# The last down projection in two column halves, with seven block products instead of eight in 15 of its 44 blocks

## The chip, the cores and the metric

One core of one Trainium2 chip runs the whole program once. The metric is the device time of one execution in microseconds (us); lower is better. The engines are called TensorE (PE in rows), VectorE (DVE), ScalarE (ACT), GpSimd (POOL) and SyncE (SP, which issues the DMAs of the weight stream).

## The reference

Two transformer blocks run over 256 tokens of width 2048, all in float32. The change lies in the end of the second block: the down projection of the SwiGLU, the residual addition and the final norm.

```python
def swiglu(h, w_in, w_down):
    gu = h @ w_in
    gate, up = jnp.split(gu, 2, axis=-1)
    return (jax.nn.silu(gate) * up) @ w_down
...
        x = x + swiglu(rmsnorm_2(x, norm_ffn_g[layer]), w_ffn_in[layer], w_ffn_down[layer])
    return rmsnorm_2(x, norm_final_g)
```

The hidden activation is 256 x 5632 and the weight `w_down` is 5632 x 2048, so the product sums over 44 slices of 128 rows.

## The kernel before

**The weight stream.** All weights are read once from HBM as one stream of pieces of 128 x 1024 float32 (512 KB). SyncE loads them in a fixed order into six raw buffers (`raw`, `RR` = 6). A buffer is loaded again when the piece that it held has been split.

**The split.** TensorE multiplies in a shortened form of float32 (`F32R`). Each piece is therefore split into two parts: ScalarE copies it into the shortened form (`split_hi`, line 444), and VectorE subtracts that from the original (`split_lo`, line 460). Both parts lie in a ring of four places (`ring`, `R` = 4). ScalarE waits for `weights_used` before it writes a place again, VectorE waits for `hi_ready`, TensorE waits for `lo_ready`. Activations are split in the same way: `hid2` holds both parts of the hidden activation.

**A block product.** `tokens` (lines 515 to 519) computes 128 tokens x 512 columns over 128 rows of the weight in three matmuls: low activation by high weight, high by low, high by high. The three lines 517, 518 and 519 are one matmul each.

**The last down projection (`down2`).** It takes 88 pieces. A piece holds two slices of 128 rows (`k`) and 512 of the 2048 columns, which makes it a *column quarter* `q`. Before, the quarters come one after the other: 22 pieces of quarter 0, then 22 of quarter 1, and so on. TensorE makes four block products for each piece, two slices by two halves of the tokens (`tt`), and sums into PSUM bank `2 * q + tt`. Piece by piece it waits for `lo_ready`. In the last quarter the last three pieces (`BY_TOKEN`) are taken for the first token half and then for the second, so that the first half can be finished earlier. TensorE also transposes the residual `x` into token order in between (`turn_x`), and ScalarE copies it out (`copy_turned`).

**After each quarter** VectorE adds the sum onto the residual in token order (`onto_tokens`, line 1742), ScalarE squares it for the norm (`square_tokens`, line 1160), and VectorE multiplies by the gain (`gained`, line 1747). These steps stand between calls of `split_lo` and `split_hi` in each engine's own order, which is written out by hand. Every engine works strictly in that order. The other engines tell each other by counting semaphores.

**GpSimd** has 30 instructions in the whole program, all in the first stage: squares of the context (lines 713 and 716), its scaling (line 722) and sums of squares (lines 726 and 730). It does nothing in the last stage.

Of the kernel before, what the change touches and what calls it, by code (L numbers as in the profile page):

```python
# [13 lines left out]
P = 128  # L14
D = 2048
T = 256
# [118 lines left out]


# [74 lines left out]
def two_blocks(nc, stream, cvec_d, c_bc_d, vecs_d, xc_d, x_d, rpb, w_fnet, base_tab, rope_tab, dft_tab, na_mask,  # L211
               stick_tab, dist_tab, g_bc_d, out_d):
    ctx = ExitStack()
    with ctx:
# [106 lines left out]
        pair2, _ = place("pair2", [P, KT, 2, T], F32R, reg)  # L321

# [80 lines left out]
        out_act, out_dve = sem("out_act"), sem("out_dve")  # L403

# [20 lines left out]
        def split_view(part, c, k, n):  # L425
            if by_tile(c):
                return split_tiles(part, c).rearrange("p (k m) n -> p k m n", k=k)
            return whole(part, c).rearrange("p (k n) -> p k n", k=k)

# [114 lines left out]
        def _(e):  # L544
# [158 lines left out]

        RES = {"out": 0, "down": 16, "out2": 32, "down2": 48}
# [26 lines left out]


        @block.scalar
        def _(e):
# [421 lines left out]
            def square_tokens(q, tt):  # L1156
                e.wait_ge(tok_y, 4 * q + 2 * tt + 1 if q < 3 else 13 + tt)
                if q:
# [4 lines left out]
            b, size = BASE["down2"], FT // 2  # L1163
            e.preload_act_table_set("sqrt_and_others")
            split_hi(e, b + LEAD + CPG, b + LEAD + 10)
            for n in range(4):
# [3 lines left out]
            split_hi(e, b + LEAD + 10, b + LEAD + 16)  # L1170
            for n in range(4, 8):
                copy_turned(n)
            at = b + LEAD + 16
            for q in range(3):
                to = b + (q + 1) * size + LEAD + 4
                split_hi(e, at, to)
                at = to
                for tt in range(2):
                    square_tokens(q, tt)
            split_hi(e, at, N_CHUNKS)  # L1180
# [12 lines left out]
        def _(e):  # L1193
# [544 lines left out]

            def onto_tokens(q, tt):
                e.wait_ge(tok_act, 2 * q + tt + 1)  # L1740
# [4 lines left out]
            def gained(q, tt):  # L1745
                e.wait_ge(tok_y, 4 * q + 2 * tt + 1)
# [3 lines left out]
            b, size = BASE["down2"], FT // 2  # L1750
            split_lo(e, b + LEAD + CPG, b + LEAD + 10)
            e.wait_ge(r_turned, 2)
            e.tensor_copy(small[:, 0:2], ps[:, 3, 0:2]).then_inc(r_copied, 1)
            at = b + LEAD + 10
            e.wait_ge(r_copied, 2)
            for q in range(3):
                to = b + (q + 1) * size + LEAD
                split_lo(e, at, to)
                at = to
                e.wait_ge(weights_used, b + (q + 1) * size)  # L1760
                if q == 0:
                    e.wait_ge(s_tables2, 48)
                for tt in range(2):
                    onto_tokens(q, tt)
                    split_lo(e, at, at + 1)
                    gained(q, tt)
                    split_lo(e, at + 1, at + 2)
                    at += 2
            split_lo(e, at, N_CHUNKS - 8)
# [6 lines left out]
            split_lo(e, N_CHUNKS - 8, N_CHUNKS)  # L1776
            for tt in range(2):
                if tt == 0:
                    e.wait_ge(column_done, COLUMN["down2"] + 1)
# [13 lines left out]
        def _(e):  # L1793
# [614 lines left out]
            def turn_x(n0):  # L2408

                e.wait_ge(sums_ready, SUMS["down2"])  # L2410
                if n0 == 0:
                    e.wait_ge(rinv_ready, NORM["ffn2"][2] + 1)
                    for tt in range(2):
                        m = e.matmul(ps[:, 3, tt:tt + 1], rinv[:, 0, tok(tt)], ident[:, 0:1], start=tt == 0, stop=True,
                                     skip_group_check=True)
                    m.then_inc(r_turned, 1)
                for n in range(n0, n0 + 4):
                    q, tt, bank = turned_at(n)
                    if n >= 4:
# [5 lines left out]
            def down_product(q, c, k, kt, tt):  # L2425
                return tokens(e, ps[:, 2 * q + tt, :], split_view(HI, c, 2, GW)[:, k], split_view(LO, c, 2, GW)[:, k],
                              hid2[:, kt, 0, tok(tt)], hid2[:, kt, 1, tok(tt)], kt == 0, kt == FT - 1)

            size = FT // 2
            for q in range(4):  # L2430
                if q == 0:
                    e.wait_ge(sums_ready, SUMS["down2"] - 4)
                elif q == 1:
                    e.wait_ge(r_copied, 2)
                elif q == 2:
                    e.wait_ge(tok_act, 8)
                for ch in range(size - (BY_TOKEN if q == 3 else 0)):
                    c = BASE["down2"] + q * size + ch
                    e.wait_ge(lo_ready, c + 1)
                    for k in range(2):  # L2440
                        if q == 0:
                            e.wait_ge(hid_lo, FT + 2 * ch + k + 1)
                        for tt in range(2):
                            r = down_product(q, c, k, 2 * ch + k, tt)
                    r.then_inc(weights_used, 1)
                    if q == 0 and ch in (6, 12):
                        turn_x(0 if ch == 6 else 4)
            e.wait_ge(lo_ready, N_CHUNKS)
            for tt in range(2):
                for ch in range(size - BY_TOKEN, size):  # L2450
                    for k in range(2):
                        r = down_product(3, BASE["down2"] + 3 * size + ch, k, 2 * ch + k, tt)
# [137 lines left out]
```

## Time and profile before

| | |
|---|---|
| median of 3 runs | 2599.76 us (2599.63 to 2601.96) |
| profiled execution | 2599.75 us, of which 2597.9 us is its span |
| TensorE busy | 2572.8 us, 99% of the span |
| VectorE busy | 1763.5 us, 68% |
| ScalarE busy | 1217.7 us, 47% |
| GpSimd busy | 33.3 us, 1% |
| mean granted clock of TensorE | 0.999 |

The span is the time from the first to the last instruction of the profiled execution. Its own time is 1.85 us longer; that part lies around the span. TensorE's busy time counts matmuls whose modelled ends overlap their successors, so it tells that the engine has work and not that it is at its peak.

### The profile page before, as it was taken

How to read it: one execution, taken by the hardware profiler on the slowest of the kernel's cores; microseconds unless marked ns; L12 is line 12 of the kernel's file. 1: busy time of each engine (PE TensorE's matmuls, PEld its weight loads, DVE VectorE, ACT ScalarE, POOL GpSimd, SP SyncE). 2: the span in 40 equal slices, each digit the busy share in tenths (PEclk: the TensorE clock that was granted, in tenths of full speed). 3: DMA queues.
4: the chain of work that ended last, by engine and by line, in shares of the span. 5: the costliest groups of instructions: out<-in, count | busy, mean ns of one | idle time of the engine just before them, and what ended most of it. 6: DMA issues, size and time to landing. Idle time of an engine off the chain costs nothing.

```text
span 2597.9 us, 36331 instructions
## 1 busy us (share of the span) xinstructions
PE 2572.8 (99%) x14852; PEld 2212.5 (85%) x14852; DVE 1763.5 (68%) x2432; ACT 1217.7 (47%) x1604; POOL 33.3 (1%) x30
## 2 busy tenths in 40 slices
PE   8999999999999999999999999999999999999998
PEld 5788788888888888888888888899888888888887
DVE  3377977888888777555756677676766666665444
ACT  4442444455555555444433555544444444444443
POOL 2100000000000000000000000000000000000000
PEclk9999999999999999999999999999999999999999
DMA  9887965677777655555555544465555555555554
GB/s 397 348 319 277 332 232 187 215 252 234 242 233 238 205 192 187 190 190 189 186 188 192 165 138 143 148 195 195 186 187 194 187 193 188 189 189 197 194 194 138
DMA packets 151414, 548.72 MB, mean 211 GB/s; under 512 B 16976, under 2 KB 18896, under 8 KB 150352
## 3 DMA queue, kind: packets, MB, share of 16 engines
q1 hardware_dynamic: 148464, 540.34, 61.8%
q10 hardware_dynamic: 2784, 6.06, 0.7%
q8 instruction: 117, 1.92, 0.3%
q14 instruction: 49, 0.40, 0.1%
HBM read 543.72 MB, written 2.10 MB: 210 GB/s over the span
## 4 chain that ended last, share of the span: by engine, by line
PE 94%; DVE 4%; DMA 1%; ACT 1%; issue 0%; ACTq 0%; SPq 0%; DVEq 0%
PE ps L507 42%; PE ps L506 21%; PE ps L519 4%; PE ps L518 4%; PE ps L517 4%; PE ps L511 3%; PE ps L504 3%; PE ps L512 3%; PE ps L513 3%; DVE raw L470 2%; PE ps L505 1%; PE ps L1809 1%; DVE ring L460 1%; PE ps L2031 1%; DMA xc<-in_xc 0%
## 5 line engine op out<-in xcount | busy, mean ns | idle before, releaser
L507 PE MATMUL ps<-pair,ring 128*128 128x512 f32 x3994 | 1390.8, 392 | 0.0
L457 DVE TENSOR_TENSOR ring<-raw,ring 128x1024 fp32r<-128x1024 f32 x648 | 789.2, 1223 | 510.4 <-ACT ring L442 508.3
L506 PE MATMUL ps<-pair,ring 128*128 128x256 f32 x3994 | 1119.4, 280 | 0.0
L442 ACT ACTIVATE ring<-raw 128x1024 fp32r<-128x1024 f32 x648 | 683.8, 1059 | 779.8 <-PE ps L507 747.3
L507 PEld LDWEIGHTS ps<-pair,ring 128*128 128x128 f32 x3994 | 749.8, 188 | 161.1
L506 PEld LDWEIGHTS ps<-pair,ring 128*128 128x128 f32 x3994 | 750.0, 188 | 6.3 <-issue 2.7
L460 DVE TENSOR_TENSOR ring<-raw,ring 128x1024 fp32r<-128x1024 f32 x167 | 203.9, 1223 | 199.5 <-ACT ring L444 199.5
L444 ACT ACTIVATE ring<-raw 128x1024 fp32r<-128x1024 f32 x167 | 176.8, 1060 | 272.4 <-PE ps L519 178.7
L507 PE MATMUL ps<-hid,ring 128*128 128x512 f32 x688 | 238.7, 392 | 0.0
L506 PE MATMUL ps<-hid,ring 128*128 128x256 f32 x688 | 192.3, 280 | 0.0
L1358 DVE TENSOR_REDUCE tmp<-ps 128x256 f32<-128x512 f32 x244 | 165.7, 684 | 0.4
L507 PEld LDWEIGHTS ps<-hid,ring 128*128 128x128 f32 x688 | 129.1, 188 | 28.4
L470 DVE CUSTOM_DVE_ANT_0 raw<-raw,c_bc 128x1024 f32<-128x1024 f32 x128 | 153.0, 1219 | 0.2 <-DMA raw<-in_stream 0.2
L517 PE MATMUL ps<-ring,hid 128*128 128x512 f32 x352 | 137.1, 390 | 0.0
L519 PE MATMUL ps<-ring,hid 128*128 128x512 f32 x352 | 137.0, 389 | 0.0
L518 PE MATMUL ps<-ring,hid 128*128 128x512 f32 x352 | 137.0, 389 | 0.0
L506 PEld LDWEIGHTS ps<-hid,ring 128*128 128x128 f32 x688 | 129.1, 188 | 0.2
L504 PE MATMUL ps<-pair,ring 128*128 128x512 f32 x262 | 95.8, 398 | 1.4 <-DVE pair L670 1.4
L511 PE MATMUL ps<-both,ring 128*128 128x512 f32 (+1 forms) x272 | 94.9, 349 | 0.8 <-DVE both L1204 0.6
L512 PE MATMUL ps<-both,ring 128*128 128x512 f32 (+1 forms) x272 | 92.4, 340 | 0.0
L513 PE MATMUL ps<-both,ring 128*128 128x512 f32 (+1 forms) x272 | 92.3, 339 | 0.0
L519 PEld LDWEIGHTS ps<-ring,hid 128*128 128x128 f32 x352 | 66.1, 188 | 13.8
(366 smaller groups left out, 2708.2 us busy)
## 6 DMA issues: line engine op xcount, KB each, us to landing
raw<-in_stream SPq DMA_DIRECT2D x983, 512.0 KB, 4.1
raw_deep<-in_stream SPq DMA_DIRECT2D x31, 512.0 KB, 8.8
xc<-in_xc SPq DMA_DIRECT2D x4, 1024.0 KB, 8.7
x<-in_x ACTq DMA_DIRECT2D x1, 2048.0 KB, 9.2
c_bc<-in_c_bc SPq DMA_DIRECT2D x1, 1024.0 KB, 6.0
bias<-in_rpb ACTq DMA_DIRECT2D x4, 256.0 KB, 4.5
g_bc<-in_g_bc ACTq DMA_DIRECT2D x1, 1024.0 KB, 5.0
out<-out_sb SPq DMA_DIRECT2D x4, 256.0 KB, 2.7
```

The source lines that it names most:

```text
L442: e.activation(split_tiles(HI, c), raw_of(p).rearrange("p (i n) -> p i n", n=P), ACT.Copy).then_inc(hi_ready, 1)
L444: e.activation(whole(HI, c), raw_of(p), ACT.Copy).then_inc(hi_ready, 1)
L457: e.tensor_tensor(split_tiles(LO, c), raw_of(p).rearrange("p (i n) -> p i n", n=P), split_tiles(HI, c).bitcast(F32), ALU.subtract).then_in ...
L460: e.tensor_tensor(whole(LO, c), raw_of(p), whole(HI, c).bitcast(F32), ALU.subtract).then_inc(lo_ready, 1)
L470: e.tensor_tensor_reduce(out=raw_of(p), in0=raw_of(p), in1=c_bc[:, (i % 2) * CH:(i % 2 + 1) * CH], scale=1.0, scalar=0.0, op0=ALU.mult, op ...
L504: e.matmul(out, whi, both_, start=True, stop=False)
L506: e.matmul(out[:, T:2 * T], wlo, act[:, 0, :], start=False, stop=False)
L507: return e.matmul(out, whi, both_, start=False, stop=last)
L511: e.matmul(out, whi, ahi, start=first, stop=False, skip_group_check=True)
L517: e.matmul(out, alo, whi, start=first, stop=False)
L518: e.matmul(out, ahi, wlo, start=False, stop=False)
L519: return e.matmul(out, ahi, whi, start=False, stop=last)
```

## The change

**Order.** The 2048 columns are taken in two halves of 1024. Within a half the pieces of its two quarters alternate, so that two pieces that follow each other hold the same 256 rows and all 1024 columns. Such a pair is a *block*, a 2 x 2 arrangement of slices by quarters; the two slices by the two token halves are the matching 2 x 2 arrangement of the activation. There are 44 blocks. Only in the last five blocks of the second half do the quarters come one after the other again.

**Seven products.** In 15 blocks (`SEVENS`) the eight block products are replaced by seven. The first half has 8 plain blocks, then seven times a seven-product block and a plain one. The second half has two plain blocks, then eight times a seven-product block and a plain one, then four plain blocks. With A11, A12 (first token half, two slices), A21, A22 (second half) and B11, B12 (first slice, two quarters), B21, B22 (second slice), the products are:

| order on TensorE | product | sum in |
|---|---|---|
| 1 | A11 B11 | M0 |
| 2 | A12 B21 | C11 |
| 3 | (A22 - A21)(B11 + B12) | M2 |
| 4 | (A12 - A22 + A21 - A11) B22 | C12 |
| 5 | (A22 - A21 + A11)(B11 + B12 + B22) | M1 |
| 6 | (A11 - A21)(B12 + B22) | M3 |
| 7 | A22 (B11 + B12 + B22 + B21) | C21 |

M0 to M3 take the four PSUM banks that the other column half leaves free.

**Operand sums.** GpSimd makes three weight sums of 128 x 512 (`weight_sums`) and five activation sums (`activation_sums`): one of 128 x 512, four of 128 x 128. VectorE makes the fourth weight sum. ScalarE copies each of them into the shortened form and VectorE makes each remainder (`seven_hi`, `seven_lo`). The buffers for the sums (`wsum14`, `wsum23`, `w_split`, `a_whole`, `a_sum`, `a_split`) exist once each.

**Folding.** Once in each half ScalarE copies M0 out of PSUM (`fold_copy`), VectorE makes four combinations of M0 to M3 (`fold_sums`) and adds four of them onto the residual (`fold_onto`), besides the four `onto_tokens` of the half.

**Stream.** The host lays the same pieces in the new order. A raw buffer that holds a piece of a seven-product block is loaded again only when `merged` has counted that block, too.

The core of the diff:

```diff
+HALVES = ([PLAIN] * 8 + [SEVEN, PLAIN] * 7, [PLAIN, PLAIN] + [SEVEN, PLAIN] * 8 + [PLAIN] * 4)
+SIDE = 17
...
                         e.wait_ge(lo_ready, i + 1)
+                        if i in SEVEN_OF:
+                            e.wait_ge(merged, KT + SEVEN_OF[i] + 1)
...
+            def weight_sums(n):
+                for col in range(2):
+                    p = POS[("weights", BASE["down2"] + SEVENS[n] + col)]
+                    e.wait_ge(landed[PLACE[p]], 16 * NTH[p])
+                if n == 0:
+                    e.wait_ge(weights_used, BASE["down2"])
+                else:
+                    e.wait_ge(wsum_lo, 3 * n)
+                e.tensor_tensor(wsum14[:, 0], seven_raw(n, 0, 0), seven_raw(n, 0, 1), ALU.add).then_inc(wsums, 1)
+                e.tensor_tensor(wsum23[:, 1], seven_raw(n, 0, 1), seven_raw(n, 1, 1), ALU.add).then_inc(wsums, 1)
+                e.wait_ge(wsums, 3 * n + 1)
+                e.tensor_tensor(wsum23[:, 0], wsum14[:, 0], seven_raw(n, 1, 1), ALU.add).then_inc(wsums, 1)
+
+            def activation_sums(n):
+                ch = LAST[SEVENS[n]][1]
+                e.wait_ge(hid_lo, FT + 2 * ch + 2)
+                if n:
+                    e.wait_ge(m_lo, KT + n)
+                h = hid2[:, 2 * ch:2 * ch + 2]
+                e.tensor_tensor(a_whole[:], h[:, :, 0].bitcast(F32), h[:, :, 1].bitcast(F32), ALU.add).then_inc(c_added, 1)
+                e.wait_ge(c_added, RT + 5 * n + 1)
+                e.tensor_tensor(a_sum[:, 0], a_whole[:, 1, P:T], a_whole[:, 0, P:T], ALU.subtract).then_inc(c_added, 1)
+                e.tensor_tensor(a_sum[:, 3], a_whole[:, 0, 0:P], a_whole[:, 0, P:T], ALU.subtract).then_inc(c_added, 1)
+                e.wait_ge(c_added, RT + 5 * n + 2)
+                e.tensor_tensor(a_sum[:, 2], a_sum[:, 0], a_whole[:, 0, 0:P], ALU.add).then_inc(c_added, 1)
+                e.wait_ge(c_added, RT + 5 * n + 4)
+                e.tensor_tensor(a_sum[:, 1], a_whole[:, 1, 0:P], a_sum[:, 2], ALU.subtract).then_inc(c_added, 1)
...
+            def seven_hi(n):
+                c = BASE["down2"] + SEVENS[n]
+                p = POS[("weights", c + 1)]
+                e.wait_ge(landed[PLACE[p]], 16 * NTH[p])
+                e.wait_ge(weights_used, c + 1 - R + 1)
+                e.activation(seven_place(n, HI, 1, 1), seven_raw(n, 1, 1), ACT.Copy).then_inc(hi_ready, 1)
+                e.wait_ge(wsums, 3 * n + 1)
+                e.activation(seven_place(n, HI, 1, 0), wsum14[:, 0], ACT.Copy).then_inc(wsum_hi, 1)
+                if n == 0:
+                    e.wait_ge(tok_turned, 8)
+                else:
+                    e.wait_ge(column_done, COLUMN["down2"] + n)
+                if n == N7[0]:
+                    e.wait_ge(resid, RES["down2"] + 4)
+                e.wait_ge(c_added, RT + 5 * n + 5)
+                e.activation(a_split[:, 0], a_sum[:], ACT.Copy).then_inc(m_hi, 1)
+                e.wait_ge(wsums, 3 * n + 3)
+                e.activation(w_split[:, HI, 0:2], wsum23[:], ACT.Copy).then_inc(wsum_hi, 1)
+                e.wait_ge(merged, KT + n + 1)
+                e.activation(w_split[:, HI, 2], wsum14[:, 1], ACT.Copy).then_inc(wsum_hi, 1)
...
+            def seven_lo(n):
+                c = BASE["down2"] + SEVENS[n]
+                e.wait_ge(hi_ready, c + 2)
+                e.tensor_tensor(seven_place(n, LO, 1, 1), seven_raw(n, 1, 1), seven_place(n, HI, 1, 1).bitcast(F32),
+                                ALU.subtract).then_inc(lo_ready, 1)
+                e.wait_ge(wsums, 3 * n + 3)
+                e.tensor_tensor(wsum14[:, 1], wsum23[:, 0], seven_raw(n, 1, 0), ALU.add).then_inc(merged, 1)
+                e.wait_ge(wsum_hi, 3 * n + 1)
+                e.tensor_tensor(seven_place(n, LO, 1, 0), wsum14[:, 0], seven_place(n, HI, 1, 0).bitcast(F32),
+                                ALU.subtract).then_inc(wsum_lo, 1)
+                e.wait_ge(m_hi, KT + n + 1)
+                e.tensor_tensor(a_split[:, 1], a_sum[:], a_split[:, 0].bitcast(F32), ALU.subtract).then_inc(m_lo, 1)
+                e.wait_ge(wsum_hi, 3 * n + 2)
+                e.tensor_tensor(w_split[:, LO, 0:2], wsum23[:], w_split[:, HI, 0:2].bitcast(F32), ALU.subtract)\
+                    .then_inc(wsum_lo, 1)
+                e.wait_ge(wsum_hi, 3 * n + 3)
+                e.tensor_tensor(w_split[:, LO, 2], wsum14[:, 1], w_split[:, HI, 2].bitcast(F32), ALU.subtract)\
+                    .then_inc(wsum_lo, 1)
...
+                if n == N7[0] - 1:
+                    split_lo(e, at, b + FT + 2)
+                    fold_sums(0)
+                    fold_onto(0, 0, 2)
+                    split_lo(e, b + FT + 2, b + FT + 3)
+                    fold_onto(0, 2, 4)
+                    split_lo(e, b + FT + 3, b + FT + 4)
+                    at = b + FT + 4
+                    e.wait_ge(weights_used, b + FT)
+                    for q, tt in ONTO[0:4]:
+                        onto_tokens(q, tt)
...
+                e.wait_ge(lo_ready, c + 1)
...
+                onto_m(0, placed(0, 0), down_act(2 * ch, 0))
+                onto_c(c11, placed(0, 1), down_act(2 * ch + 1, 0)).then_inc(weights_used, 1)
+                e.wait_ge(lo_ready, c + 2)
+                e.wait_ge(wsum_lo, 3 * n + 1)
+                e.wait_ge(m_lo, KT + n + 1)
+                onto_m(2, placed(1, 0), act_sum(0))
+                onto_c(c12, placed(1, 1), act_sum(1)).then_inc(weights_used, 1)
+                e.wait_ge(wsum_lo, 3 * n + 2)
+                onto_m(1, summed(0), act_sum(2))
+                onto_m(3, summed(1), act_sum(3))
+                e.wait_ge(wsum_lo, 3 * n + 3)
+                onto_c(c21, summed(2), down_act(2 * ch + 1, 1)).then_inc(column_done, 1)
```

## Rows read from the trace of the kernel before

**Rows 1.** The page: busy time, share and instructions of each engine.
```profile
PE 2572.8 (99%) x14852; PEld 2212.5 (85%) x14852; DVE 1763.5 (68%) x2432; ACT 1217.7 (47%) x1604; POOL 33.3 (1%) x30
```

**Rows 2.** Busy time by stretch: us, busy (instructions), granted clock, DMA share, GB/s.
```profile
2400.00:2450.00 50.00, 50.00 (x222) 41.42 (x221) 24.58 (x22) 21.13 (x23) 0.00 (x0) 1.00 0.58 191
```

**Rows 3.** Who waited for whom from 2400 to 2560 us, all engines.
```profile
ACT ring L444 <- PE ps L519: 94.0, 59, 1.7
DVE ring L460 <- ACT ring L444: 80.4, 59, 1.5
```

**Rows 4.** Timeline of VectorE: start, us, engine, line.
```profile
2376.77 2.36 DVE L460 TENSOR_TENSOR ring<-raw,ring 128x1024 fp32r<-128x1024 f32 x2 [1.85 <-ACT ring L444]
...
2461.16 1.23 DVE L460 TENSOR_TENSOR ring<-raw,ring 128x1024 fp32r<-128x1024 f32 x1 [1.49 <-ACT ring L444]
2463.88 1.22 DVE L460 TENSOR_TENSOR ring<-raw,ring 128x1024 fp32r<-128x1024 f32 x1 [1.50 <-ACT ring L444]
```

**Rows 5.** Groups by form, 2355 to 2598 us: busy us, mean ns, idle before.
```profile
L444 ACT ACTIVATE ring<-raw 128x1024 fp32r<-128x1024 f32 x82 | 87.0, 1061 | 129.7 <-PE ps L519 129.7
...
L1742 DVE SCALAR_TENSOR_TENSOR x_tok<-ps,small,x_tok 128x512 f32<-128x512 f32 x8 | 6.0, 746 | 5.2 <-PE ps L519 5.2
...
L1747 DVE TENSOR_TENSOR out_sb<-x_tok,g_bc 128x512 f32<-128x512 f32 x6 | 4.1, 684 | 0.0
L1154 ACT ACTIVATE x_tok<-ps 128x512 f32<-128x512 f32 x8 | 4.1, 594 | 0.0
```

**Rows 6.** Groups by form of the whole program, ScalarE and VectorE.
```profile
L1145 ACT ACTIVATE pair<-gates 128x512 fp32r<-128x512 f32 x8 | 4.9, 634 | 12.6 <-DVE gates L1726 12.6
...
L1731 DVE TENSOR_TENSOR pair<-gates,pair 128x512 fp32r<-128x512 f32 x8 | 5.2, 690 | 0.9 <-ACT pair L1145 0.9
```

**Rows 7.** Groups by form of GpSimd, whole program.
```profile
L722 POOL TENSOR_TENSOR tmp<-xc,rinv 128x512 f32<-128x512 f32 x16 | 21.2, 1326 | 79.3 <-DVE both L1204 70.8 <-DVE rinv L1214 8.5
...
L2580 POOL MEMSET const-float32-0.0<- 128x1 f32 x1 | 0.1, 98 | 0.2 <-issue 0.2
```

**Rows 8.** Timeline of GpSimd: first stage.
```profile
9.90 1.04 POOL L713 TENSOR_TENSOR tmp<-xc 128x512 f32<-128x512 f32 x1 [1.46 <-DMA xc<-in_xc]
11.02 1.27 POOL L716 TENSOR_TENSOR tmp<-tmp 128x512 f32<-128x512 f32 x1
12.42 1.31 POOL L713 TENSOR_TENSOR tmp<-xc 128x512 f32<-128x512 f32 x1
13.81 1.59 POOL L716 TENSOR_TENSOR tmp<-tmp 128x512 f32<-128x512 f32 x1
23.89 3.28 POOL L722 TENSOR_TENSOR tmp<-xc,rinv 128x512 f32<-128x512 f32 x2 [8.48 <-DVE rinv L1214]
...
141.01 4.16 POOL L730 TENSOR_TENSOR sq_acc<-sq_acc,sq_slot 128x512 f32<-128x512 f32 x3 [0.98 <-ACT sq_slot L785]
```

**Rows 9.** Timeline of VectorE over the same times.
```profile
11.04 1.79 DVE L1211 TENSOR_TENSOR sq_acc<-sq_acc,sqx_home 128x512 f32<-128x512 f32 x1 [1.29 <-ACT sqx_home L758]
12.97 2.99 DVE L1211 TENSOR_TENSOR sq_acc<-sq_acc,sqx_cbc 128x512 f32<-128x512 f32 x2
...
24.92 1.04 DVE L1198 SCALAR_TENSOR_TENSOR first_gain<-first_mod,vecs 128x2 f32<-128x2 f32 x1
...
98.38 0.16 DVE L1198 SCALAR_TENSOR_TENSOR first_gain<-first_mod,vecs 128x2 f32<-128x2 f32 x1
...
141.55 0.75 DVE L1231 SCALAR_TENSOR_TENSOR ckvn<-ps,vecs,ckvn 128x512 fp32r<-128x512 f32 x1 [0.31 <-ACT ckvn L786]
```

**Rows 10.** Busy time by stretch at the end, columns as in rows 2.
```profile
2590.00:2591.00 1.00, 0.58 (x3) 0.15 (x1) 0.38 (x1) 0.00 (x0) 0.00 (x0) 1.00 0.64 240
...
2593.00:2594.00 1.00, 0.00 (x0) 0.00 (x0) 0.83 (x2) 0.83 (x1) 0.00 (x0) 0.71 0.06 18
2594.00:2595.00 1.00, 0.00 (x0) 0.00 (x0) 0.00 (x0) 0.00 (x0) 0.00 (x0) 0.50 0.75 281
```

**Rows 11.** Timeline at the start of the last three pieces.
```profile
2582.12 0.19 PEld L517 LDWEIGHTS ps<-ring,hid 128*128 128x128 f32 x1 [0.17 <-DVE ring L460]
```

More of the change, by code:

```diff
@@ L134 @@
 OM_ORDER = {0: 1, 2: 2, 1: 3, 3: 4}
+PLAIN, SEVEN = 0, 1
+HALVES = ([PLAIN] * 8 + [SEVEN, PLAIN] * 7, [PLAIN, PLAIN] + [SEVEN, PLAIN] * 8 + [PLAIN] * 4)
+SIDE = 17
+LAST = []
+for _h, _kinds in enumerate(HALVES):
+    assert len(_kinds) == FT // 2
+    for _ch, _kind in enumerate(_kinds):
+        if _h == 0 or _ch < SIDE:
+            LAST.extend((2 * _h + _q, _ch, _kind) for _q in range(2))
+LAST.extend((_q, _ch, PLAIN) for _q in (2, 3) for _ch in range(SIDE, FT // 2))
+assert len(LAST) == 2 * FT and SEVEN not in HALVES[1][SIDE:]
+SEVENS = [_i for _i, (_q, _ch, _kind) in enumerate(LAST) if _kind == SEVEN and _q % 2 == 0]
+N7 = (HALVES[0].count(SEVEN), len(SEVENS))
+SEVEN_OF = {BASE["down2"] + _i + _k: _n for _n, _i in enumerate(SEVENS) for _k in range(2)}
+ONTO = [(0, 0), (1, 0), (0, 1), (1, 1), (2, 0), (2, 1), (3, 0), (3, 1)]
+TOK_Y = [1, 2, 3, 4, 9, 11, 13, 14]
 SUMS = {}
@@ L428, in split_view, with seven_raw, seven_place @@
             return whole(part, c).rearrange("p (k n) -> p k n", k=k)
+        def seven_raw(n, row, col):
+            v = raw_of(POS[("weights", BASE["down2"] + SEVENS[n] + col)])
+            return v[:, row * GW:(row + 1) * GW]
+        def seven_place(n, part, col, k):
+            return whole(part, BASE["down2"] + SEVENS[n] + col)[:, k * GW:(k + 1) * GW]
         def split_hi(e, a, b):
@@ new lines, in fold_onto @@
+            def fold_onto(h, a, b):
+                for i, (q, tt) in [(f - 4 * h, at) for at, f in FOLDED.items()][4 * h + a:4 * h + b]:
+                    if i == 0 and h == 0:
+                        e.wait_ge(tok_act, 8)
+                    if i:
+                        e.wait_ge(sums_ready, SUMS["down2"] + 4 * h + i + 1)
+                    v = columns(x_tok, tt, q)
+                    e.scalar_tensor_tensor(out=v, in0=fold[:, i + (i > 0)], scalar=small[:, tt:tt + 1], in1=v, op0=ALU.mult,
+                                           op1=ALU.add).then_inc(resid, 1)
@@ L1754, in _ @@
-            at = b + LEAD + 10
+            e.tensor_copy(small[:, 0:2], ps[:, 7, 0:2]).then_inc(r_copied, 1)
             e.wait_ge(r_copied, 2)
[L1756 to L1768, printed above, removed]
@@ L1770, in _ @@
+            split_lo(e, b + 2 * FT - 4, b + 2 * FT - 2)
+            e.wait_ge(weights_used, b + 2 * FT - 5)
+            for tt in range(2):
+                onto_tokens(2, tt)
+                split_lo(e, b + 2 * FT - 2 + tt, b + 2 * FT - 1 + tt)
+                gained(2, tt)
             e.wait_ge(tok_act, 14)
@@ new lines, in _ @@
+            e.wait_ge(sums_ready, SUMS["down2"] - 4)
+            i = 0
+            while i < 2 * FT - BY_TOKEN:
+                if i == 7:
+                    turn_r()
+                    turn_x(0, 3)
+                elif i == 11:
+                    turn_x(3, 6)
+                elif i == 14:
+                    turn_x(6, 8)
+                elif i == FT:
+                    e.wait_ge(sums_ready, SUMS["down2"] + 4)
+                if i in SEVENS:
+                    seven_products(SEVENS.index(i))
+                    i += 2
+                else:
+                    plain_chunk(i)
+                    i += 1
@@ L2448, in _ @@
             e.wait_ge(lo_ready, N_CHUNKS)
             for tt in range(2):
[L2450 removed]
+                for i in range(2 * FT - BY_TOKEN, 2 * FT):
                     for k in range(2):
[L2452 removed]
+                        r = down_product(i, k, tt)
                 if tt == 0:
```

179 lines of the change are left out of this document (127 added, 52 removed).

## The prediction

> **What bounds the kernel now.** I read the page first, for the busy shares. TensorE has work for 99% of the span, and GpSimd has almost none [rows 1]. The mean granted clock is 0.999, so TensorE runs at 2.4 GHz, the upper of its two levels. Then the last stage alone: in 50 us of it TensorE has no gap [rows 2]. The view of who waited for whom has no row in which TensorE waits; ScalarE waits for TensorE to free a place of the ring, and VectorE waits for ScalarE [rows 3]. So TensorE sets the pace here and the two others follow it.
>
> The pace is read from VectorE's timeline: the remainders of two pieces start 2461.16 and 2463.88, a piece every 2.72 us [rows 4]. A piece is 12 matmuls, so one takes 2.72 / 12 = 0.2267 us (the durations in the rows of matmuls overlap and are not used). A block of two pieces takes 5.44 us. Of each 2.72 us VectorE uses 1.23 us and ScalarE 1.06 us [rows 4, 5].
>
> **What the change removes.** A seven-product block has 21 matmuls instead of 24, which saves 3 x 0.2267 = 0.68 us, and 15 blocks save 10.2 us if TensorE never waits. The other matmuls, the transposes and the bytes of the stream stay the same. A different order of pieces costs nothing as such: the DMA share is 0.58 here [rows 2].
>
> **What it adds in one period.** From one seven-product block to the next there is one plain block between. TensorE's work in that period is 21 + 24 = 45 matmuls, 10.20 us, where before it was 10.88 us. The others get:
>
> - VectorE: three whole remainders (the plain block's two pieces, and the first piece of the seven-product block), then 128 x 512 operations four times (remainder of B22, fourth weight sum, remainder of B11 + B12, remainder of the four activation sums), one of 128 x 1024 and one more of 128 x 512 for the other weight sums. A whole one takes 1.23 us alone and 1.13 us when it follows another (2.36 - 1.23) [rows 4]. One of 128 x 512 takes 0.69 us [rows 6], about 0.60 in sequence if it overlaps its successor by the same 0.1 us. Together 4 x 1.13 + 5 x 0.60 = 7.5 us.
> - ScalarE: 3 x 1.06 + 1.06 + 4 x 0.63 = 6.8 us [rows 5, 6].
> - GpSimd: four sums of 128 x 512, 1.27 us each alone [rows 8], and four of 128 x 128. No row shows such a small one. Below, it costs a quarter, 0.32 us; above, a whole 1.27 us. A fill of one element takes 0.10 us [rows 7]; taking that as the fixed part, 0.10 + 1.17 / 4 = 0.4 us. I take 0.4, since the fill is the nearest row to a small operation. Together 6.7 us.
>
> Each engine alone would fit in 10.2 us. Two things break that.
>
> **First: GpSimd and VectorE exclude each other.** The first stage shows both at once [rows 8, 9]. At 11.02 a GpSimd sum starts and ends at 12.29. VectorE's sum of 128 x 512 starts at 11.04 and takes 1.79 instead of 0.69 us: it ends 12.83, 0.54 us after GpSimd. The GpSimd square that starts at 12.42 takes 1.31 us instead of the 1.04 us of its twin at 9.90. The next two VectorE sums take 2.99 us together and end 15.96, again 0.56 us after the GpSimd sum that ran to 15.40. That one held VectorE off from 14.27 (12.42 + 1.31 + 0.54) for 1.13 us. At 24.92, in the middle of GpSimd's pair from 23.89 on, even an operation of two elements takes 1.04 us instead of 0.16. A VectorE operation that reads one of its tensors from PSUM is not hit: 0.75 us while GpSimd runs three sums at its usual 1.3 to 1.4 us each [rows 8, 9]. All of VectorE's operations in the period read two tensors from SBUF, so they cannot lie beside GpSimd's. The prices while both have work are 1.10 us (whole) and 0.55 us (half) for VectorE, 1.13 us for GpSimd's large sums.
>
> The Trainium skill has this as a rule (SBUF — State Buffer, section "SBUF: two separate sides"): the port pair shared by VectorE and GpSimd is an exclusive lock, held for the whole instruction, and a VectorE operation with two SBUF inputs takes it against a GpSimd one. The rows agree on the exclusion but show 1.13 of 1.27 us and 0.54 of 0.69 us as the part that excludes. By whole instructions the period below would be 1.4 us longer, and the time some 2668 us.
>
> **Second: the work is a chain.** GpSimd starts the sums of block n only after VectorE's last remainder of block n - 1 (`wsum_lo`), because the buffers exist once. The activation copy waits for all of GpSimd's sums, and behind it come the last copies and remainders. From one last remainder to the next:
>
> 1. Until GpSimd's last sum both engines share one door. VectorE does three whole remainders and three half operations, 3 x 1.10 + 3 x 0.55 = 4.95 us. GpSimd does 4 x 1.13 + 4 x 0.40 = 6.1 us. Together 11.05 us, in whatever order they take turns.
> 2. ScalarE copies the activation sums, 0.63 us [rows 6], then the two weight sums, 1.0 us in sequence [rows 5]; VectorE's activation remainder lies beside that.
> 3. VectorE makes the remainder of these, 1.23 us, then the last one, 0.60 us.
>
> That is 11.05 + 3.45 = 14.5 us. TensorE needs 10.2 of it and waits 4.3 us, because its products 3 to 7 need what steps 2 and 3 make. Behind the waiting operations stand the next pieces' copies and remainders in the same queues, so nothing can run ahead. Against 10.88 us before, a period loses 3.6 us.
>
> **The sum.** There are 6 such periods in the first half and 7 in the second: 13 x (14.5 - 10.88) = +47.1 us. The first seven-product block has eight plain ones ahead of it and only gains: -0.7 us.
>
> Between the halves lie three plain blocks and the folding. VectorE has there six whole remainders (6.8), four fold sums (0.68 each, 2.7), four additions from SBUF (0.7 each, 2.8), four from PSUM (0.75, 3.0), and the block's 1.1 + 3 x 0.6 + 0.6 + 1.2 + 0.6 = 5.3: 20.6 us, with the waits for column and copy about 22. Of GpSimd's 6.1 us some 3.5 can lie beside operations from PSUM; 2.6 are added. That makes 24.7 us, against 8 x 2.72 = 21.8 before: +2.9 us.
>
> After the last seven-product block come ten pieces, 27.2 us for TensorE. VectorE has ten remainders (11.4 to 12), the folding (5.5), five gains (0.69 each [rows 5]) and two additions (0.75 each [rows 5]) before the last remainder: 21.9 us after the last weight remainder of the block. TensorE starts products 5 to 7 some 0.5 us before that point and is through 9 matmuls, 2.04 us, later, at 1.55; it reaches the last three pieces, which need VectorE's last remainder, at 1.55 + 7 x 2.72 = 20.6 us. It waits 1.3 us instead of the 0.17 us of before [rows 11]: +1.1 us. The steps after the last matmul are unchanged.
>
> Sum: 47.1 - 0.7 + 2.9 + 1.1 = +50.4 us. The profiled execution took 2599.75 us (its span of 2597.9 and 1.85 around it), which is the median of the runs to 0.01 us. That gives 2650 us.
>
> **Unknown costs.** The four small sums: at 0.32 us the period is 0.3 us shorter, at 1.27 us each 3.5 us longer (+45 us in all). The activation sum reads 2 x 256 elements in two runs; no row has that form, and I take the plain price, with the same upper end. The handoffs: none in the sum; a GpSimd sum that waits for the one before it starts 0.08 us after its end (9.90 + 1.04 to 11.02 [rows 8]), and six or so such steps in a chain would add 0.5 us a period, +6 us. If VectorE's remaining work in step 1 can run beside GpSimd's waits for its own results, a period loses up to 1 us, -13 us.
>
> **Rivals.**
>
> - *The two engines do not hold each other up here.* For it: the rows of exclusion are few and from another stage; against it: every overlapping pair with two SBUF inputs shows it. Then the chain is GpSimd 6.7 + 0.4 for handoffs, copies 1.6, remainders 1.9: 10.7 us. Periods give 13 x (10.7 - 10.88) = -2.3 us, with -0.7, +0.4 and +1.1 it is -1.5: 2598 us, within 0.2%. Chance 0.05.
> - *The change pays (the other side).* TensorE paces the periods: that needs the chain to be at most 10.2 us, that is step 1 at most 6.75 us instead of 11.05, so no exclusion and GpSimd sums of at most 1.15 us. Then -10.2 + 1.3 = -9 us: 2591 us. Any chain over 10.88 us per period turns the sign. Chance 0.04.
> - *Partly hidden:* the exclusion holds but some of step 1 or 2 hides, periods of 11.5 to 13.5 us: +12 to +38 us, 2612 to 2638 us. Chance 0.2.
> - *Dearer small sums or handoffs:* periods of 16 to 18 us, +70 to +96 us: 2670 to 2696 us. Chance 0.2.
> - *TensorE's clock falls.* Its wait in a period is in one piece, about 4 us ahead of product 3. At the end the granted clock is 0.5 (1.2 GHz) 2.5 to 3.5 us after the last matmul [rows 10]. Slow products 3 to 7 cost 15 x 0.2267 = 3.4 us more, and the 4.3 us of waiting absorb that. But if the clock stayed low, TensorE would need 20.4 us a period: +124 us, about 2727 us. Chance 0.04. The Trainium skill (TensorE: Matmul & The Clock Gate, section "Why this matters for your kernels") warns that gaps between bursts of matmuls throttle the clock; no row of before shows such bursts in a steady stage.
>
> The forecast itself, periods of 13.5 to 16 us, has 0.47.
>
> **The numbers.** 2650 us. The range takes in the partly hidden case and the dearer one up to about 17.3 us per period: 2612 to 2688 us. A measurement of this kernel can tell 0.2%, about 5 us, from no change. Faster by more: 0.05 (2591 and part of 2598's spread); within: 0.05; slower: 0.90.
>
> **What would show it.** In the changed profile VectorE's remainders of plain pieces take up to 2.3 us where GpSimd runs, and 1.23 elsewhere; GpSimd's large sums take up to 2.3 us. TensorE waits in each period, for VectorE's activation or weight remainder, 4 us or so in one piece, and its granted clock dips. `column_done` repeats every 14.5 us. No matmul waits for a DMA. I am wrong if TensorE shows no gaps between seven-product blocks, or if operations of both engines overlap at their usual durations.

## The result, and the profile after

The changed kernel takes 2651.28 us (median of 5 runs, 2649.41 to 2656.24), the one before 2599.76 us (5 runs, 2598.57 to 2601.96). The ratio is 1.020, with an interval of 1.0185 to 1.0215: slower, by 51.5 us where 50.4 us were forecast. The profiled execution took 2649.41 us, the shortest of the five; its span is 2647.5 us, 49.6 us longer than before.

The page of the changed kernel: its line of busy shares, then four of its 40-slice lines. They answer to [rows 1].

```profile
PE 2583.3 (98%) x14807; PEld 2213.8 (84%) x14807; DVE 1880.9 (71%) x2523; ACT 1246.4 (47%) x1666; POOL 194.9 (7%) x150
...
PE   8999999999999999999999999999999999998878
...
DVE  3377967888888776556665776776666666668887
...
POOL 2100000000000000000000000000000000007673
PEclk9999999999999999999999999999999999999989
```

The only new thing sits in the last four slices: GpSimd works, VectorE is busier, and TensorE is no longer full. The slices are 66 us long, so the stage must be read by itself. This is the timeline of GpSimd over one period of the second half (start, us, engine, line):

```profile
2536.93 1.28 POOL L775 TENSOR_TENSOR wsum<-raw 128x512 f32<-128x512 f32 x1 [3.70 <-DVE w_split L1862]
2538.17 2.27 POOL L776 TENSOR_TENSOR wsum<-raw 128x512 f32<-128x512 f32 x1
2540.39 2.28 POOL L778 TENSOR_TENSOR wsum<-wsum,raw 128x512 f32<-128x512 f32 x1
2542.65 2.27 POOL L786 TENSOR_TENSOR a_whole<-hid 128x512 f32<-128x512 f32 x1
...
2547.59 0.45 POOL L793 TENSOR_TENSOR a_sum<-a_whole,a_sum 128x128 f32<-128x128 f32 x1
```

And this is VectorE over the same period of the changed kernel:

```profile
2536.07 0.69 DVE L1862 TENSOR_TENSOR w_split<-wsum,w_split 128x512 fp32r<-128x512 f32 x1
2537.01 6.76 DVE L492 TENSOR_TENSOR ring<-raw,ring 128x1024 fp32r<-128x1024 f32 x3 [0.25 <-ACT ring L476]
2543.69 1.77 DVE L1849 TENSOR_TENSOR ring<-raw,ring 128x512 fp32r<-128x512 f32 x1
...
2548.80 0.69 DVE L1857 TENSOR_TENSOR a_split<-a_sum,a_split 128x512 fp32r<-128x512 f32 x1 [1.60 <-ACT a_split L1247]
2549.74 1.23 DVE L1859 TENSOR_TENSOR w_split<-wsum,w_split 128x1024 fp32r<-128x1024 f32 x1 [0.25 <-ACT w_split L1249]
2550.89 0.68 DVE L1862 TENSOR_TENSOR w_split<-wsum,w_split 128x512 fp32r<-128x512 f32 x1
```

Three whole remainders take 6.76 us, where two in sequence took 2.36 us before [rows 4]. GpSimd's large sums take 2.27 us when they have to wait for VectorE and 1.28 us when they do not. From one last remainder (L1862) to the next are 14.82 us. Up to the end of GpSimd's last sum it is 2548.04 - 2536.76 = 11.28 us (forecast 11.05); from there to the last remainder's end, 2551.57, it is 3.53 us (forecast 3.45).

TensorE's side, by the view of who waited for whom in the changed kernel, 2400 to 2645 us (us in total, times, longest):

```profile
ACT a_split L1247 <- POOL a_sum L793: 106.1, 14, 8.3
...
PE ps L549 <- DVE a_split L1857: 37.9, 14, 4.3
```

ScalarE waits for GpSimd's last activation sum, and TensorE for the remainder of the activation sums, once in each block from the second on.

VectorE's timeline gives the decomposition. These are the starts of the last weight remainder of the first, second, seventh, eighth and fifteenth block:

```profile
2393.54 0.68 DVE L1862 TENSOR_TENSOR w_split<-wsum,w_split 128x512 fp32r<-128x512 f32 x1
...
2408.22 0.69 DVE L1862 TENSOR_TENSOR w_split<-wsum,w_split 128x512 fp32r<-128x512 f32 x1
...
2481.51 0.69 DVE L1862 TENSOR_TENSOR w_split<-wsum,w_split 128x512 fp32r<-128x512 f32 x1
...
2506.17 0.68 DVE L1862 TENSOR_TENSOR w_split<-wsum,w_split 128x512 fp32r<-128x512 f32 x1
...
2609.80 0.68 DVE L1862 TENSOR_TENSOR w_split<-wsum,w_split 128x512 fp32r<-128x512 f32 x1
```

| stretch | measured | before, pieces of 2.72 us | difference | forecast |
|---|---|---|---|---|
| six periods of the first half, 14.66 each | 88.0 | 65.3 | +22.7 | +21.7 |
| between the halves | 24.7 | 21.8 | +2.9 | +2.9 |
| seven periods of the second half, 14.80 on average | 103.6 | 76.2 | +27.5 | +25.3 |
| all ahead of and behind these (the remainder of 49.6) | | | -3.5 | +0.4 |

### The profile page after: what moved, and what is told of

Same layout as the page of the kernel before. It is cut to its first block, busy times and chain, and to the rows that moved or that the text cites. A ratio compares the mean times of both kernels' runs of the same rounds, so it can differ in the third digit from the quotient of the medians.

```text
span 2647.5 us, 36602 instructions
## 1 busy us (share of the span) xinstructions
PE 2583.3 (98%) x14807; PEld 2213.8 (84%) x14807; DVE 1880.9 (71%) x2523; ACT 1246.4 (47%) x1666; POOL 194.9 (7%) x150
## 4 chain that ended last, share of the span: by engine, by line
PE 85%; DVE 7%; POOL 4%; issue 2%; ACT 1%; DMA 1%; ACTq 0%; SPq 0%; POOLq 0%
PE ps L539 41%; PE ps L538 21%; PE ps L543 3%; PE ps L536 3%; PE ps L545 3%; PE ps L544 3%; PE ps L549 2%; PE ps L551 2%; PE ps L550 2%; DVE ring L492 2%; DVE raw L502 1%; PE ps L537 1%; POOL wsum L778 1%; PE ps L1973 1%; POOL wsum L775 1%
## 5 line engine op out<-in xcount | busy, mean ns | idle before, releaser
L489 DVE TENSOR_TENSOR ring<-raw,ring 128x1024 fp32r<-128x1024 f32 x648 | 789.3, 1224 | 510.3 <-ACT ring L474 508.2
L474 ACT ACTIVATE ring<-raw 128x1024 fp32r<-128x1024 f32 x648 | 683.7, 1059 | 779.8 <-PE ps L539 747.3
L492 DVE TENSOR_TENSOR ring<-raw,ring 128x1024 fp32r<-128x1024 f32 x152 | 216.9, 1444 | 99.6 <-ACT ring L476 99.4
L476 ACT ACTIVATE ring<-raw 128x1024 fp32r<-128x1024 f32 x152 | 157.3, 1054 | 171.2 <-PE ps L551 78.0
L775 POOL TENSOR_TENSOR wsum<-raw 128x512 f32<-128x512 f32 x15 | 29.7, 1977 | 2298.4 <-DMA raw<-in_stream 2242.9
L549 PE MATMUL ps<-ring,hid 128*128 128x512 f32 x262 | 102.7, 392 | 1.9 <-DVE ring L492 1.9
L551 PE MATMUL ps<-ring,hid 128*128 128x512 f32 x262 | 102.0, 389 | 0.0
L550 PE MATMUL ps<-ring,hid 128*128 128x512 f32 x262 | 102.0, 389 | 0.0
```

What stands on the lines that cost most here:

```text
L474: e.activation(split_tiles(HI, c), raw_of(p).rearrange("p (i n) -> p i n", n=P), ACT.Copy).then_inc(hi_ready, 1)
L476: e.activation(whole(HI, c), raw_of(p), ACT.Copy).then_inc(hi_ready, 1)
L489: e.tensor_tensor(split_tiles(LO, c), raw_of(p).rearrange("p (i n) -> p i n", n=P), split_tiles(HI, c).bitcast(F32), ALU.subtract).then_in ...
L492: e.tensor_tensor(whole(LO, c), raw_of(p), whole(HI, c).bitcast(F32), ALU.subtract).then_inc(lo_ready, 1)
```

## The experiments

**Sums of 8 columns.** It asks whether the loss lies in GpSimd's sums at all.

```diff
-                e.tensor_tensor(wsum14[:, 0], seven_raw(n, 0, 0), seven_raw(n, 0, 1), ALU.add).then_inc(wsums, 1)
+                e.tensor_tensor(wsum14[:, 0, 0:8], seven_raw(n, 0, 0)[:, 0:8], seven_raw(n, 0, 1)[:, 0:8], ALU.add).then_inc(wsums, 1)
... (the other seven sums alike)
```

> The changed kernel, but GpSimd's eight sums per seven-product block cover 8 columns instead of 512 or 128; the sum buffers are filled with zeros once before. This leaves out nearly all of the operand sums, so the output is not the reference's; every wait and every other instruction stays. Theory (GpSimd's sums and VectorE exclude each other, and the sums stand in a chain): without the sums the chain is VectorE's 5.2 us plus 3.5 us plus eight short operations, under TensorE's 10.2 us a period, so TensorE has no waits in the periods, its granted clock stays 1.00, and the time is 2590 to 2592 us. Rival (the loss is in the seven products, the folding, the new order or in TensorE's clock): the time stays above 2600 us.

Measured: 2590.46 us in one run. From 2400 to 2450 us TensorE has no gap and the granted clock is 1.00. So the seven products, the folding, the new order and all the waits cost nothing by themselves: with GpSimd's sums all but gone, the arithmetic of the change gives its 9 to 10 us. The whole loss of 61 us against this run comes with the length of eight GpSimd operations per block.

**Fills instead of sums.** It keeps the time that GpSimd takes and the chain, and takes away that it reads.

```diff
+            def fill(v):
+                count[0] += 1
+                e.memset(v, 0.0).then_inc(filled, 1)
+                e.wait_ge(filled, 5 + count[0])
+                return e.memset(v, 0.0)
...
-                e.tensor_tensor(wsum14[:, 0], seven_raw(n, 0, 0), seven_raw(n, 0, 1), ALU.add).then_inc(wsums, 1)
+                fill(wsum14[:, 0]).then_inc(wsums, 1)
... (the other seven alike)
```

> The changed kernel, but each of GpSimd's sums is replaced by two fills of the same output with zeros, one after the other, which read nothing. It leaves out the operand sums, so the output is not the reference's. From the rows of before a pair takes 0.52 + 0.08 + 0.52 = 1.1 us for 512 elements (the sum 1.27) and about 0.2 + 0.08 + 0.2 = 0.5 us for 128 (the last sum of a block took 0.46 us). So GpSimd has nearly the same time to itself in the chain. Theory, if only operations that read SBUF exclude VectorE: remainders keep 1.23 us, the chain is 7.1 + 3.5 = 10.6 us a period, the time 2595 to 2600 us. Theory, if fills exclude it as well: VectorE's remainders are stretched and the time is over 2630 us. Rival (the chain of waits alone makes the periods long, whoever holds what): the same chain with the same durations gives 2645 us or more with remainders at 1.23 us.

Measured: 2592.63 us in one run. GpSimd's timeline of the kernel with fills shows a pair in 1.11 us, back to back, beside VectorE's work:

```profile
2541.54 0.53 POOL L774 MEMSET wsum<- 128x512 f32 x1
2542.01 0.53 POOL L772 MEMSET a_whole<- 128x512 f32 x1
2542.59 0.53 POOL L774 MEMSET a_whole<- 128x512 f32 x1
```

VectorE's timeline of the same kernel:

```profile
2539.14 1.23 DVE L493 TENSOR_TENSOR ring<-raw,ring 128x1024 fp32r<-128x1024 f32 x1 [0.43 <-ACT ring L477]
2541.87 2.58 DVE L493 TENSOR_TENSOR ring<-raw,ring 128x1024 fp32r<-128x1024 f32 x2 [1.50 <-ACT ring L477]
2544.37 0.69 DVE L1858 TENSOR_TENSOR ring<-raw,ring 128x512 fp32r<-128x512 f32 x1
```

The view of line 493 of the same kernel, 2400 to 2560 us, has the shortest, the middle and the longest of the 47 whole remainders in nanoseconds:

```profile
L493 DVE TENSOR_TENSOR ring<-raw,ring x47: 1211/1225/1227, 2399.7 to 2558.8; 128x1024 fp32r<-128x1024 f32 x47
```

Neither engine is stretched. GpSimd's eight results take 6.1 us here, and the next block's begin 3.7 us after their end: 9.8 us from block to block, which hides under TensorE's 10.2 us. The time is 2.4 us below the expected 2595 us, because GpSimd's part is 1 us shorter than the 7.1 us taken there. The waits are the same as in the changed kernel; GpSimd's time is less than 1 us a period below its own 6.9 us (4 x 1.27 + 4 x 0.46). By this estimate a chain alone would need some 10.6 us with real sums, not 14.7. So some 4 us of each period are the mutual exclusion. It comes with the sums, which read SBUF, and not with the fills, which only write. The Trainium skill (SBUF — State Buffer, section "SBUF: two separate sides") says just that: a VectorE operation with two SBUF inputs is blocked only by a GpSimd operation that reads SBUF. A sum differs from a fill in its arithmetic, too; no run here has a GpSimd operation that computes without reading SBUF, so it is the page, and not a run, that puts it down to the reading.

**All sums on VectorE.**

```diff
             def seven_lo(n):
                 c = BASE["down2"] + SEVENS[n]
+                weight_sums(n)
+                activation_sums(n)
...
-            for n in range(N7[1]):          (GpSimd)
-                weight_sums(n)
-                activation_sums(n)
```

> The changed kernel with all eight sums of a block made by VectorE, at the head of its own sequence for the block; GpSimd does nothing in this stage. Theory: VectorE then has 7.5 us plus 4 x 0.60 plus 4 x 0.28 = 11.0 us a period and some drains, 11.2 to 11.7 us, and nothing blocks it. Against 14.7 us a period the helper costs more than it gives: the time falls to 2601 to 2612 us. Rival (GpSimd takes real work off VectorE, and the stretch has another cause): VectorE's 11.7 us of stretched work plus 3.5 us makes the periods as long or longer, 2650 us or more.

Measured: 2601.7 us, ratio 1.0006 (0.9997 to 1.0015): as fast as before, 50 us faster than with the helper. VectorE's timeline of this kernel, the same operation one period apart and a small sum:

```profile
2536.40 0.69 DVE L1833 TENSOR_TENSOR a_whole<-hid 128x512 f32<-128x512 f32 x1
2537.13 0.29 DVE L1835 TENSOR_TENSOR a_sum<-a_whole 128x128 f32<-128x128 f32 x1
...
2547.43 0.68 DVE L1833 TENSOR_TENSOR a_whole<-hid 128x512 f32<-128x512 f32 x1
```

The period is 11.03 us, and VectorE has work for 49.65 of the 50 us from 2400 on. TensorE waits a little in each: it has work for 49.01 of them. By the sum of the prices (11.0 - 7.5) the eight sums cost VectorE 3.5 us. On GpSimd, exclusion made 4.2 us of each period (11.28 + 3.53 less the 10.6 us of the chain without it). This period is still over 10.88, so 15 blocks with one plain block between do not pay this way either.

**Activation sums early.**

```diff
+            activation_sums(0)
             for n in range(N7[1]):
                 weight_sums(n)
-                activation_sums(n)
+                if n + 1 < N7[1]:
+                    activation_sums(n + 1)
```

> The changed kernel with the five activation sums of the next block issued on GpSimd as soon as VectorE has the remainder of this block's, ahead of the next weight sums. All work stays. Theory: the chain is shorter (the activation copy waits no more at its end), but both engines still share one door: VectorE 4 x 1.10 + 5 x 0.55 = 7.2 and GpSimd 4 x 1.13 + 4 x 0.35 = 5.9 us, 13.1 us less what falls into idle handoffs; periods of 12.2 to 13.2 us, 2620 to 2633 us, still slower than before. Rival (a chain of waits without exclusion): the chain loses GpSimd's activation part of about 3.5 us, periods of 11.2 us or less, 2600 to 2608 us.

Measured: 2635.86 us, ratio 1.0137 (1.012 to 1.0154), just above the range. Periods are 13.49 us (VectorE's last remainders start 2528.01 and 2541.50), 1.2 to 1.3 us shorter, but for the first of the second half with 14.43 us. The rival without exclusion gave 2608 us at most. The period is over the expected 13.2 us because the new order makes another chain: VectorE stands idle 3.7 us a period until GpSimd's weight sums are there, and GpSimd 2.1 us until VectorE's activation remainder:

```profile
2538.55 0.69 DVE L1854 TENSOR_TENSOR wsum<-wsum,raw 128x512 f32<-128x512 f32 x1 [3.67 <-POOL wsum L778]
```

**Both: early sums and two sets of buffers.**

```diff
+        wsum14s = [place(f"wsum14_{i}", [P, 2, GW], at=both_at + (20 - 4 * i) * K1)[0] for i in range(2)]
+        wsum23s = [place(f"wsum23_{i}", [P, 2, GW], at=both_at + (28 - 4 * i) * K1)[0] for i in range(2)]
...
-                else:
-                    e.wait_ge(wsum_lo, 3 * n)
+                elif n > 1:
+                    e.wait_ge(wsum_lo, 3 * (n - 1))
```

> The early activation sums of the run before, and two sets of buffers for the weight sums, so that GpSimd makes the weight sums of block n while VectorE is still at block n - 1. All work stays, and hardly any wait between the two is left. Theory (one door): the floor is what both hold it for, VectorE 4 x 1.07 + 5 x 0.54 = 7.0 and GpSimd 4 x 1.13 + 4 x 0.33 = 5.8 us, so periods of 12.6 to 13.2 us and 2620 to 2632 us, only 0.3 to 0.9 us a period under the 13.49 us of the early sums alone. Rival (what was left there is still the chain of waits): periods at TensorE's 10.2 or VectorE's 7.5 to 8.4 us of own work, 2588 to 2600 us.

Measured: 2636.22 us, ratio 1.0138 (1.0125 to 1.0152), the same as without the second set, and periods of 13.48 us. Neither theory's number came. The run tests nothing new: in this order the activation sums of the next block stand ahead of its weight sums and wait for VectorE, so the second set is never used early, and VectorE's 3.67 us of idle time are still there.

**Two sets, the changed kernel's order.** The same buffers without the early sums.

> Two sets of buffers for the weight sums as before, but in the changed kernel's own order on GpSimd: weight sums, then activation sums. In the run with both edits the activation sums of block n + 1 stood ahead of its weight sums and waited for VectorE, so the second set was never used early. Here the weight sums of block n start while VectorE waits for ScalarE in block n - 1. Theory (one door, 7.0 + 5.8 us): 12.8 to 13.4 us a period, 2623 to 2633 us. Rival (only a chain): 11 us a period or less, 2605 us or less.

Measured: 2628.45 us, ratio 1.0109 (1.0094 to 1.0124). VectorE's last remainders start 2502.10 for the eighth block and 2590.98 for the fifteenth, seven periods of 12.70 us on average; the single ones are uneven, 9.7 to 15.4 us. The sum of what both hold the door for is 12.8 us. Now even the remainders late in the block, which had 1.23 us in the changed kernel, are stretched, as VectorE's timeline of this kernel shows:

```profile
2524.93 2.31 DVE L1862 TENSOR_TENSOR w_split<-wsum,w_split 128x1024 fp32r<-128x1024 f32 x1
2527.16 1.78 DVE L1865 TENSOR_TENSOR w_split<-wsum,w_split 128x512 fp32r<-128x512 f32 x1
```

So freeing this wait brings the mean period from 14.7 to 12.7 us, which is about the sum of what both hold the door for. It lies 1.8 us above the 10.88 us of plain blocks.

**One seven-product block in each half.**

```diff
+HALVES = ([PLAIN] * 8 + [SEVEN] + [PLAIN] * 13, [PLAIN, PLAIN, SEVEN] + [PLAIN] * 19)
```

> The changed kernel with only one seven-product block in each half, the first; the order of the pieces, the folding and GpSimd's sums for these two stay, and the four squares stand later on ScalarE. This prices the order and the folding. Theory (order and folding cost nearly nothing, and each block stands alone behind plain ones): -1.4 us for the two blocks, +0.5 to +1.5 us at the end: 2598.5 to 2600.5 us. Rival (the column halves or the folding carry part of the loss): 2603 us or more.

Measured: 2600.29 us, ratio 1.0001 (0.9992 to 1.001). The order in column halves and the folding are free within what can be told, some 2 us.

**Two plain blocks between, sums on VectorE.**

```diff
+HALVES = ([PLAIN] * 8 + [SEVEN, PLAIN, PLAIN] * 4 + [SEVEN, PLAIN], [PLAIN, PLAIN] + [SEVEN, PLAIN, PLAIN] * 5 + [PLAIN] * 5)
```

> All sums on VectorE, and two plain blocks between seven-product blocks instead of one, so 10 such blocks instead of 15. Theory: VectorE needs 11.02 us for a seven-product and a plain block (measured with the sums on it) and 2.3 us more for the second plain one, 13.3 us, where TensorE needs 69 matmuls, 15.6 us. TensorE paces, and each seven-product block gives its 0.68 us: -6.8 us, and +0.5 to +2 us for folding, the stretch between the halves and the end: 2593.5 to 2596 us. Rival (seven products cost something else that the lighter load does not remove): 2599 us or more.

Measured: 2595.72 us, ratio 0.9982 (0.9973 to 0.9991), within the range. TensorE has work without a gap from 2400 to 2450 and from 2500 to 2550 us, and the periods there are 15.63 to 15.65 us: its own pace.

**Twelve blocks, one and two plain ones between in turn, sums on VectorE.**

> As the spaced one, but with one and two plain blocks between in turn, 12 seven-product blocks. Theory: two of them and three plain blocks cost VectorE 2 x 8.75 + 3 x 2.27 = 24.3 us and TensorE 25.8 us; the short gap leaves TensorE 0.8 us behind, the long one gives VectorE it back. If the ring carries that, -8.2 us and +0.5 to +3 us: 2592 to 2595 us; if it does not, each short gap costs 0.8 us and it is 2595 to 2600 us.

Measured: 2594.50 us, ratio 0.9980 (0.9971 to 0.9989). The time alone cannot tell the two cases apart, since its runs lie between 2593.93 and 2596.76 us. The trace can: short periods of 11.02 us and long ones of 14.85 to 15.74 us alternate, and TensorE has no gap from 2400 to 2450 and from 2500 to 2550 us. The ring carries it.

**Two plain blocks between, sums on GpSimd, activation sums early.**

> Two plain blocks between seven-product blocks (10 of them) with the sums on GpSimd, activation sums early. Theory: one more plain block adds 2.2 us of VectorE's hold, so the 13.49 us of the early order become 15.7 us against TensorE's 15.64 us: the blocks gain their 0.68 us each and lose about 0.1 to 0.4 us again: 2594 to 2600 us. Rival (GpSimd's sums cost a fixed stall per block, whatever lies between): 10/15 of the loss stays, 2620 us or more.

Measured: 2594.83 us, ratio 0.9980 (0.9971 to 0.999). The periods are 15.4 to 15.6 us with one of 16.5, about TensorE's 15.64 us for 69 matmuls, and TensorE has work for 99.6 of the 100 us from 2400 to 2450 and from 2500 to 2550. So the stall is not a fixed price per block: the same exclusion is there, and costs nothing once 15.6 us are there to hold what both engines need.

These three beat both kernels. They are 0.2% faster than the one before, and among themselves they cannot be told apart.

## Why the prediction was right

- **What bounds the stage, and the 0.68 us per block.** Right. With the sums all but gone the time is 2590.46 us; the text gave 2591 us for TensorE pacing every period.
- **Exclusion, read from the first stage.** Right, also in its prices. The experiments isolate it: fills of nearly the same length give 2592.63 us, real sums 2651.28 us. It was taken from a handful of coincidences in another stage, and it made 4 of the 14.5 us. By the Trainium skill (SBUF — State Buffer, section "SBUF: two separate sides") the lock is held for the whole instruction; with the rows' durations that gives, as an estimate, 15.9 us a period and 2668 us. The 14.6 to 14.8 us measured in 12 of the 13 periods stand with the shorter hold from the rows: the measurement decides.
- **The chain.** Right: 11.28 + 3.53 us in the trace for 11.05 + 3.45. The second set of buffers shows its share: 14.7 to 12.7 us.
- **The periods in detail.** In all the 13 periods cost 3.1 us more than 13 x 14.5. The small sum on GpSimd, taken as 0.40 us, is 0.46 us alone but holds VectorE up for only about 0.32 us, so that GpSimd's share of step 1 comes out as the forecast 6.1 us. What was missing are the handoffs, which the sum had at nothing: 0.08 us before GpSimd's last sum, 0.08 us in steps 2 and 3, and, where VectorE has nothing to do meanwhile, 0.17 us before GpSimd's first sum. The first half's periods are 14.65 to 14.68 us. In the second half ScalarE's squares stand ahead of the next copies in four periods, 14.80 to 14.82 us each, and not in the last two, 14.64 and 14.65. The first one there is 15.10 us, because GpSimd's first sum got no turn for so long (see the last section).
- **The head start of the first block** was left out. In the first block VectorE's last remainder ends 2394.2 and TensorE's last matmul of product 7 starts only at 2398.6; in the second block the two are 2408.9 and 2410.3. VectorE had eight plain blocks to get ahead, and the first of the 13 periods used that up: TensorE lost 3 us less than 13 full periods. The two errors, +3 us in the periods and -3 us here, cancel; the closeness of 2650 to 2651 us is partly luck.
- **Between the halves**: the sum is right, 24.66 us for the forecast's 24.7, and its terms are not. VectorE never waited there (about 1.4 us were forecast), and its unstretched work was somewhat cheaper. But GpSimd held it up for about 4.8 us and not 2.6: the four additions from SBUF took 6.2 us instead of 2.8, and two whole remainders 2.31 and 1.48 us. Its sums came mostly beside these. It was idle beside the fold sums, and only one small sum started beside the four additions from PSUM. There neither was stretched, as the split by operands said. Timeline of the changed kernel, VectorE first, then GpSimd:

```profile
2489.17 3.55 DVE L1882 SCALAR_TENSOR_TENSOR x_tok<-fold,small,x_tok 128x512 f32<-128x512 f32 x2
...
2498.86 2.71 DVE L1888 SCALAR_TENSOR_TENSOR x_tok<-ps,small,x_tok 128x512 f32<-128x512 f32 x4
```

```profile
2499.33 0.46 POOL L793 TENSOR_TENSOR a_sum<-a_whole,a_sum 128x128 f32<-128x128 f32 x1
```

- **The end**: forecast 1.3 us of waiting before the last three pieces, measured 0.77. TensorE's weight loads in the changed kernel:

```profile
2631.68 0.19 PEld L549 LDWEIGHTS ps<-ring,hid 128*128 128x128 f32 x1 [0.77 <-DVE ring L492]
```

- **The clock.** The wait in each period is in one piece as foreseen, but 1.2 to 4.3 us, on average 2.7 (37.9 us in 14 waits), and not 4: TensorE comes later to it where the products of the block before were slow. Busy time by stretch in the changed kernel (columns as in [rows 2]):

```profile
2546.00:2548.00 2.00, 0.88 (x4) 0.38 (x3) 1.20 (x2) 0.00 (x0) 1.92 (x3) 1.00 0.30 57
2548.00:2550.00 2.00, 0.36 (x1) 0.40 (x2) 0.95 (x2) 1.86 (x3) 0.04 (x1) 0.76 0.97 389
2550.00:2552.00 2.00, 2.00 (x6) 1.52 (x6) 1.75 (x3) 2.00 (x5) 0.26 (x1) 0.50 0.19 78
2552.00:2554.00 2.00, 2.00 (x9) 1.60 (x8) 2.00 (x1) 2.00 (x3) 2.00 (x2) 0.89 0.00 0
```

The granted clock is 1.00, TensorE stops, the clock falls to 0.50 (1.2 GHz) and is back at 1.00 by 2554. Six of the fifteen matmuls of products 3 to 7 run in the slow part here, and the fifteen take 4.8 us instead of 3.4; in the other blocks it is none to twelve, 3.4 to 5.9 us. It costs nothing, by the trace: in the second block the clock stayed at 1.00 through them and the period behind it is 14.66 us; in the seventh it was 0.50, and the periods on either side of such blocks are 14.65 to 14.67 us all the same, because TensorE still waits for VectorE. The rival of a clock that stays low did not come.

- **A slip in a rival.** For two engines that do not hold each other up the text adds 6.7 + 0.4 + 1.6 + 1.9 to 10.7 us. It is 10.6, and the rival's time 2597 us instead of 2598; that changes nothing in the forecast.

The measured periods lie in the forecast's own case, 13.5 to 16 us, which had the chance 0.47.

## What to carry to other kernels

An idle GpSimd is not free help for VectorE. In this kernel's traces a GpSimd sum from SBUF and a VectorE operation with two SBUF inputs take turns, so their times must be added and compared with the period of the engine that paces: here 7.0 + 5.8 us against 10.2 us, while each alone would have fitted. Sums of 0.69 us on VectorE cost less than the 1.28 us on GpSimd that hold VectorE up for 1.13.

Before a saving of TensorE's time is paid with operand work, the neighbours' work per saved product has to fit in the pace everywhere, not on average over the stage: seven-product blocks with two plain ones between, ten instead of fifteen, gain 4 to 6 us instead of losing 50. And a coincidence of two engines anywhere in the old trace, even in a stage that the change does not touch, is worth reading for its durations.

## What the runs showed of the hardware

- Turns are not always fair. In the steady periods the two engines alternate, operation by operation. But when GpSimd came with the first sum of the ninth block, VectorE went on for four operations, and the sum of 1.28 us took 4.99 us. Timeline of the changed kernel, VectorE first:

```profile
2506.77 3.48 DVE L492 TENSOR_TENSOR ring<-raw,ring 128x1024 fp32r<-128x1024 f32 x3
2510.18 0.68 DVE L1849 TENSOR_TENSOR ring<-raw,ring 128x512 fp32r<-128x512 f32 x1
```

and GpSimd:

```profile
2507.02 4.99 POOL L775 TENSOR_TENSOR wsum<-raw 128x512 f32<-128x512 f32 x1 [7.22 <-DVE w_split L1862]
```

It ends 2512.01, 1.15 us after VectorE's last one. In the run with both edits one such sum took 6.74 us. What decides it is open. That VectorE ran without a break before is not enough: it did so for 4.4 us before the second block's first sum, too, which came at 2394.39 and took 2.12 us, a wait for one operation.

- A GpSimd fill of 128 x 512 takes 0.53 us with VectorE's two-input operations beside it and 0.52 without: writing alone is not held up.
- A GpSimd sum of 128 x 128 takes 0.46 us, 36% of the 1.28 us of one four times as long; on VectorE it is 0.29 of 0.69 us.
